# Decoder block on one core: the expert loop's gather in bf16 parts, norm weights behind it, residual in the last block

## The reference

```python
h = h + token_mixer(rmsnorm(h, norm_mix_w), ...)
xn = rmsnorm(h, norm_ffn_w)
logits = xn @ w_router + b_router
top_v, top_i = lax.top_k(logits, 4); gates = softmax(top_v)
# for each expert e, over the tokens routed to it:
hgu = x_e @ w_gate_up[e] + b_gate_up[e]          # 1024 -> 2048
act = min(g, 7) * sigmoid(1.702 * min(g, 7)) * (clip(u, -7, 7) + 1)
y_e = act @ w_down[e] + b_down[e]                # 1024 -> 1024
h = h + sum over experts of gate * y_e
out = rmsnorm(h, norm_final_w)[:, 16:]
```

## Time and profile before

| | |
|---|---|
| median of 3 executions | 1346.57 us |
| the profiled execution, its device time | 1345.64 us |
| its span, first to last instruction | 1343.9 us |
| TensorE matmul busy | 1329.1 us (99%) |
| VectorE busy | 567.4 us (42%) |
| ScalarE busy | 287.4 us (21%) |
| HBM read | 466.41 MB |
| granted TensorE clock, mean | 0.997 |

### The profile page before, as it was taken

How to read it: one execution, slowest core, us unless ns; L and a number is a source line. 1 busy time by engine, 2 the same in 40 slices (tenths; PEclk the granted TensorE clock), 3 DMA queues, 4 the chain that set the end, 5 groups by cost and what they waited for, 6 DMA issues and landing times.

```text
span 1343.9 us, 20286 instructions
## 1 busy us (share of the span) xinstructions
PE 1329.1 (99%) x8121; PEld 785.9 (58%) x8121; DVE 567.4 (42%) x1101; ACT 287.4 (21%) x500; POOL 14.3 (1%) x33
## 2 busy tenths in 40 slices
PE   8999999999999999999999999999999999999997
PEld 8999889899985444444444454444444444444442
DVE  5897899875645232232222232222232222232222
ACT  5443344443541011011011011011011011011011
POOL 1000000000000000000000000000000000000000
PEclk9999999999999999999999999999999999999999
DMA  9653353356678899999999999999999999999993
GB/s 326 223 165 121 129 180 126 126 189 192 219 302 334 378 418 432 431 433 432 430 433 432 430 433 434 429 432 434 429 433 433 430 432 433 430 432 425 428 428 150
DMA packets 77159, 467.91 MB, mean 348 GB/s; under 512 B 4295, under 2 KB 62199, under 8 KB 63335
## 3 DMA queue, kind: packets, MB, share of 16 engines
q1 hardware_dynamic: 76736, 467.32, 84.9%
q10 hardware_dynamic: 391, 0.16, 0.0%
HBM read 466.41 MB, written 1.05 MB: 348 GB/s over the span
## 4 chain that ended last, share of the span: by engine, by line
PE 97%; DVE 1%; ACT 1%; ACTq 0%; issue 0%; DVEq 0%
PE pb L754 33%; PE pb L781 17%; PE pb L719 9%; PE pb L529 6%; PE pb L531 6%; PE pb L530 6%; PE pb L804 5%; PE pb L690 2%; PE pb L773 2%; PE pb L796 1%; PE pb L761 1%; PE pb L771 1%; PE pb L494 1%; PE pb L614 1%; PE pb L616 1%; PE pb L615 1%
## 5 line engine op out<-in xcount | busy, mean ns | idle before, releaser
L1542 DVE TENSOR_SCALAR work<-pb 64x512 f32<-64x512 f32 x64 | 43.7, 683 | 480.7 <-PE pb L761 480.7
L754 PE MATMUL pb<-work,ubuf 128*64 128x512 f32 x992 | 218.1, 592 | 0.0
L529 PE MATMUL pb<-parts,whi 128*128 128x256 f32 (+1 forms) x640 | 185.3, 290 | 0.7 <-DVE parts L1137 0.7
L531 PE MATMUL pb<-parts,wlo 128*128 128x256 f32 (+1 forms) x640 | 182.5, 285 | 0.0
L530 PE MATMUL pb<-parts,whi 128*128 128x256 f32 (+1 forms) x640 | 182.3, 285 | 0.0
L754 PEld LDWEIGHTS pb<-work,ubuf 128*64 128x64 f32 x992 | 70.3, 137 | 132.9 <-issue 132.8
L1126 DVE TENSOR_TENSOR wlo<-work,whi 128x1024 fp32r<-128x1024 f32 x104 | 126.4, 1219 | 49.7 <-ACT whi L908 49.5
L908 ACT ACTIVATE whi<-work 128x1024 fp32r<-128x1024 f32 x104 | 109.4, 1057 | 135.6 <-PE pb L531 107.0
L781 PE MATMUL pb<-work,ubuf 128*64 128x512 f32 x576 | 130.6, 595 | 0.1
L754 PE MATMUL pb<-late_w,ubuf 128*64 128x512 f32 x576 | 126.7, 592 | 0.0
L719 PEld LDWEIGHTS pb<-onehot,hw 128*128 128x128 f32 x992 | 113.1, 192 | 19.4 <-issue 19.4
(11 more groups left out here) (235 smaller groups left out, 1324.2 us busy)
## 6 DMA issues: line engine op xcount, KB each, us to landing
work<-in_w_gate_up SPq DMA_DIRECT2D x28, 4096.0 KB, 21.6
split_w<-in_w_gate_up SPq DMA_DIRECT2D x15, 4096.0 KB, 21.1
late_w<-in_w_gate_up SPq DMA_DIRECT2D x14, 4096.0 KB, 21.1
work<-in_w_down SPq DMA_DIRECT2D x14, 4096.0 KB, 17.9
work<-in_w_in SPq DMA_DIRECT2D x40, 1024.0 KB, 5.2
late_w<-in_w_down SPq DMA_DIRECT2D x7, 4096.0 KB, 18.4
split_w<-in_w_down SPq DMA_DIRECT2D x7, 4096.0 KB, 18.7
late_w<-in_w_gate_up SPq DMA_DIRECT2D x8, 2048.0 KB, 17.7
```

The source lines that it names most:

```text
L529: pe.matmul(o, wh, xh, start=first, stop=False)
L531: ins = pe.matmul(o, wl, xh, start=False, stop=last)
L754: ins = pe.matmul(pb[u * SLOTS:(u + 1) * SLOTS, bank, :], xT[:, 2 * i + k, :], w[:, k, u * HID:(u + 1) * HID], start=(i == 0 and k == 0), ...
L1542: dve.tensor_scalar(hg, pb[0:SLOTS, 4 + s, :], LIMIT, None, ALU.min).then_inc(min_rdy, 1)
```

## The change

1. `hw` is kept as three bf16 parts whose sum is the float32 value: x3[0] = bf16(hw), x3[1] = bf16(hw - x3[0]), x3[2] = the rest. The loop's `gather` uses the three parts and a bf16 one-hot matrix: 6 matmuls into each of 8 column ranges in place of 2, all in bf16. The parts are made in the front by ScalarE (`first_part`, `second_part`) and VectorE (`rest_of`, `third_part`). `gather_first` stays in float32.
2. The norm's weights are no longer in `hw`. They are multiplied in behind the gather, in the copy from PSUM (`tokens`, now a multiply with `fnw`), and for block 0 by two more multiplies. The DMA that broadcasts these weights and VectorE's multiply with them (L1389) are gone.
3. `hidden(0)` of block 0 starts its first two chunks when the first half of `xT` is ready (`xh_rdy`).
4. The residual matmuls move from ahead of the loop to the last block, behind `down_bias`. The first scatter clears the banks instead.
5. The two matmuls that count tokens (L811, L812) move ahead of `gather_first(1)`, in the place of two of the matmuls that only keep TensorE busy.
6. The first four blocks are written out; TensorE's loop over known blocks has 6 rounds instead of 7.
7. The last `w_down` pair of 2 MB is two loads of 1 MB, each with its own semaphore.
8. The last scatter signals after each token tile, and ScalarE squares tile 0 as soon as that is there.

```diff
-            sp.dma_start(nwb[:, 0, :], a["norm_ffn_w"][0:1, :].to_broadcast([P, D])).then_inc(nwb_in, 16)
...
-            reload(rounds, 6, el, w_dn, 2)
+            sp.wait_ge(w_used, LOADS * rounds + (FIXED * LOADS - 2 * AHEAD + 6 + 2))
+            for i in range(2):
+                sp.dma_start(place_at(AHEAD + 6 + i), expert_src(el, w_dn, 0)[:, (2 + i) * 2 * D:(3 + i) * 2 * D]).then_inc(end_in[i], 16)
...
             def gather():
 
                 for k in range(KC):
-                    for t in range(TT):
-                        ins = pe.matmul(pb[:, 7, k * SLOTS:(k + 1) * SLOTS], hw[:, t, k * P:(k + 1) * P], onehot[:, t, :],
-                                        start=(t == 0), stop=(t == TT - 1))
+                    for n in range(3 * TT):
+                        ins = pe.matmul(pb[:, 7, k * SLOTS:(k + 1) * SLOTS], x3[:, n % 3, n // 3, k * P:(k + 1) * P],
+                                        onehot[:, n // 3, :], start=(n == 0), stop=(n == 3 * TT - 1))
                 ins.then_inc(gathered, 1)
...
+            def add_residual():
+                for t in range(TT):
+                    for c in range(2):
+                        pe.matmul(pb[:, 2 * t + c, :], ident[:, :], hx[:, t, c * 512:(c + 1) * 512],
+                                  start=False, stop=False, skip_group_check=True)
+
-            def scatter(stop):
+            def scatter(start=False, stop=False):
+
                 for t in range(TT):
                     for c in range(2):
                         rows = slice(c * SLOTS, (c + 1) * SLOTS)
                         ins = pe.matmul(pb[:, 2 * t + c, :], hotT[rows, t * P:(t + 1) * P], ysb[rows, :],
-                                        start=False, stop=stop, skip_group_check=True)
+                                        start=start, stop=stop, skip_group_check=True)
+                    if stop:
+                        ins.then_inc(acc_done, 1)
                 return ins
...
             pe.wait_ge(table_done, 4)
-            pe.wait_ge(h2_done, 4)
-            for t in range(TT):
-                for c in range(2):
-                    pe.matmul(pb[:, 2 * t + c, :], ident[:, :], hx[:, t, c * 512:(c + 1) * 512],
-                              start=True, stop=False, skip_group_check=True)
...
+            def first_part(t):
+                sc.wait_ge(xf_rdy, t + 1)
+                sc.activation(x3[:, 0, t, :], hw[:, t, :], ACT.Copy).then_inc(x3_rdy, 1)
+
+            def second_part(t, of):
+                sc.wait_ge(xr_rdy, 2 * t + 1)
+                sc.activation(x3[:, 1, t, :], of, ACT.Copy).then_inc(x3_rdy, 1)
...
+            def rest_of(t, to, parts):
+
+                dve.wait_ge(x3_rdy, parts)
+                dve.tensor_tensor(to, hw[:, t, :], x3[:, 0, t, :], ALU.subtract).then_inc(xr_rdy, 1)
+
+            def third_part(t, of, parts):
+                dve.wait_ge(x3_rdy, parts)
+                dve.wait_ge(xr_rdy, 2 * t + 1)
+                dve.tensor_tensor(x3[:, 2, t, :], of, x3[:, 1, t, :], ALU.subtract).then_inc(xr_rdy, 1)
...
             def tokens(n):
                 dve.wait_ge(gathered, n)
-                dve.tensor_copy(xT, pb[:, 7, :].rearrange("p (k n) -> p k n", n=SLOTS)).then_inc(xt_rdy, 1)
+                dve.tensor_tensor(xT, pb[:, 7, :].rearrange("p (k n) -> p k n", n=SLOTS), fnw(0, KC), ALU.mult).then_inc(xt_rdy, 1)
...
+            rest_of(1, hw[:, 1, :], 3)
             further_blocks()
+            third_part(1, hw[:, 1, :], 4)
```

More of the change, by code:

```diff
@@ L223, in build_block @@
         e_in = [sem(f"e_in{s}") for s in range(PLACES // 4)]
+        end_in = [sem(f"end_in{i}") for i in range(2)]
         l_in = [sem(f"l_in{s}") for s in range(LOADS // 2)]
@@ L710, in _ @@
             pe.matmul(pb[:, 1, 0:NE], before[:, :], mask[:, 1, :], start=False, stop=True).then_inc(rank_done, 1)
-            keep_busy(2, 2)
+            pe.matmul(pb[:, 0, NE:2 * NE], ones[:, :], mask[:, 0, :], start=True, stop=False, skip_group_check=True)
+            pe.matmul(pb[:, 0, NE:2 * NE], ones[:, :], mask[:, 1, :], start=False, stop=True,
+                      skip_group_check=True).then_inc(rank_done, 1)
             gather_first(1, 3, 0).then_inc(first_done, 1)
@@ L740, in first_unit, with hidden @@
                 return place_at(n)
-            def hidden(s, at, n0, sel, n=None, tokens=None):
+            def hidden(s, at, n0, sel, n=None, first=False):
                 bank = 4 + s
@@ L747, in hidden @@
                     pe.wait_ge(clip_rdy, n)
-                if tokens is not None:
-                    pe.wait_ge(xt_rdy, tokens)
                 for i in range(4):
+                    if first and i == 0:
+                        pe.wait_ge(xh_rdy, 1)
+                    if first and i == 2:
+                        pe.wait_ge(xt_rdy, 1)
                     w = at(n0 + i).rearrange("p (k n) -> p k n", k=2)
@@ L809, in _, with first_half @@
             pe.wait_ge(zeroed, 1)
-            pe.matmul(pb[:, 0, NE:2 * NE], ones[:, :], mask[:, 0, :], start=True, stop=False, skip_group_check=True)
-            pe.matmul(pb[:, 0, NE:2 * NE], ones[:, :], mask[:, 1, :], start=False, stop=True,
-                      skip_group_check=True).then_inc(rank_done, 1)
-            hidden(0, first_unit, 0, 1, tokens=1)
+            hidden(0, first_unit, 0, 1, first=True)
             pe.wait_ge(table_done, 4)
-            pe.wait_ge(h2_done, 4)
-            for t in range(TT):
-                for c in range(2):
-                    pe.matmul(pb[:, 2 * t + c, :], ident[:, :], hx[:, t, c * 512:(c + 1) * 512],
-                              start=True, stop=False, skip_group_check=True)
             rounds = pe.value_load(nblocks[0:1, 0:1], min_val=NE - 1 - FIXED, max_val=MAXB - 2 - FIXED)
             last = pe.value_load(nblocks[0:1, 1:2], min_val=NE - 1, max_val=MAXB - 2)
-            def first_half(b, at, more):
+            def first_half(b, at, more, first=False):
                 hidden(1, at, 0, b + 1, 2 * b + 1)
@@ L827, in first_half @@
                     pe.wait_ge(hot_rdy, 2 * b + 4)
+                    if first:
+                        pe.wait_ge(xr_rdy, 4)
                     gather()
@@ L830, in first_half @@
                 pe.wait_ge(y_rdy, b + 1)
-                scatter(False).then_inc(scat_done, 1)
+                scatter(start=first).then_inc(scat_done, 1)
                 pe.wait_ge(min_rdy, 2 * b + 2)
@@ L839, in first_half @@
                 down_bias()
+                if not more:
+                    add_residual()
             def second_half(b, at, n0):
@@ L848, in second_half, with whole @@
                 down(1, at, n0 + 2, 1)
-            def whole(b, at):
-                first_half(b, at, True)
+            def whole(b, at, first=False):
+                first_half(b, at, True, first)
                 pe.wait_ge(gslot_rdy, b + 1)
@@ L854, in whole @@
                 second_half(b, at, 8)
-            with pe.Fori(0, FIXED // 4) as g:
+            for j in range(4):
+                whole(j, fixed_unit(0, j), first=(j == 0))
+            with pe.Fori(0, FIXED // 4 - 1) as g:
                 for j in range(4):
-                    whole(4 * g + j, fixed_unit(g, j))
+                    whole(4 * g + (4 + j), fixed_unit(g, 4 + j))
             with pe.Fori(0, rounds) as i:
                 whole(i + FIXED, later_unit(i))
-            first_half(last, later_unit(rounds), False)
-            second_half(last, later_unit(rounds), 4)
+            first_half(last, last_unit(rounds), False)
+            second_half(last, last_unit(rounds), 4)
             pe.wait_ge(hotT_rdy, last + 2)
             pe.wait_ge(y_rdy, last + 2)
-            scatter(True).then_inc(acc_done, 1)
+            scatter(stop=True)
         @block.scalar
@@ L1049, in _ @@
             normalize(0)
+            first_part(0)
             evacuate(1, 0)
+            second_part(0, rest)
             square_half(1)
@@ L1439, in _ @@
             dve.tensor_scalar(stat[:, 14:15], stat[:, 2:3], 1.0 / D, EPS, ALU.mult, ALU.add).then_inc(half_done, 1)
+            rest_of(0, rest, 1)
             choose(0)
+            third_part(0, rest, 2)
             settle(0)
```

49 lines of the change are left out of this document (30 added, 19 removed).

## The result

The changed kernel takes 1338.93 us (median of 5 executions, 1337.53 to 1341.32) against 1346.36 us of the kernel before (median of 5, 1345.65 to 1346.72): a ratio of 0.9945 [0.9931, 0.9960], 0.55% faster. The profiled execution took 1337.71 us, its span 1335.8.

A forecast was written before the change was run, and what follows sets the result against it. The prediction took the DMA stream of weight loads, 29.18 us a block, as the bound once TensorE's reserve is used up. Terms -7.6 and -1.0 sum to -8.6, giving 1338.0 us, range 1334.8 to 1342.3.

The forecast's parts named there:

- Two clocks, the stream the slower: Loop: loads need 29.18 us a block, TensorE 28.84; TensorE's work counts only until its reserve is gone, then the stream's start.
- Gather 2.98 us: Loop's gather: 48 bf16 pairs at 62 ns take 2.98 us a block instead of 3.71, saving 0.73.
- weights cost nothing: Rival on the gather's bf16 pairs: stream starts up to 1.7 us earlier, total 1336.3 to 1336.9; chance 0.12.
- TensorE 28.1 a block, waits of about 1.1 from block 14: Loop: TensorE uses 1.07 us of reserve a block, then waits a little over 1 us at each hidden(1).
- Residual's removal 3.5: Start, block 0: residual's 3.63 us gone, 3.5 counted as saved, up to 1 less if register reads show.
- 0.37 earlier for hidden(0): Start, block 0: hidden(0) needs only the first half of xT, so begins at about 408.95 instead of 409.32.
- its result is needed only behind the scatter: Loop, tokens as a multiply from PSUM: costs about what the copy did, needed only behind scatter (1.99 us) and transposes.
- 4.6 earlier for the stream: Loop's start: load issued at 441.86 goes 0.37 + 3.5 + 0.73 = 4.6 us earlier, and all landings behind it.
- Residual at the end +3.43, less 0.43 and 0.25 for two waits that go: Last block: residual adds 3.43 us; waits ahead of first down chunk (0.43) and second turn_act (0.25) are saved.
- Tail 1.0: Kernel's end: last scatter releases tile 0 at its half, so ScalarE's squares start sooner, 1.0 us saved.
- a pair of 81 ns: Rival on the gather: it takes 3.89 us, 0.18 longer, 31 times, total 1350.1; chance 0.07.
- the late one-hot rows: Rival at the start: register reads exposed and one-hot rows or parts late, 1 to 3.5 us, 1339 to 1341.5; chance 0.09.

The follow-up runs named there:

- e11: Changed kernel with 128 instead of 64 moving columns in 42 of the gather's 48 matmuls, same instruction count: 1339.32 us.
- e4: Changed kernel with only 7/8 of each 4 MB load from the sixth on, the rest stale: 1276.73 us.
- e5: Changed kernel with VectorE copying the gathered tokens before the second activation instead of after it: 1339.31 us.
- e3: Changed kernel with every gather matmul done twice, the second time over the first: 1348.58 us.
- e2: Changed kernel with the residual's matmuls back ahead of the loop: 1337.86 us.
- e6: Changed kernel with the residual's matmuls in block 3 instead of the last block: 1338.34 us.
- e9: Changed kernel with one signal after the whole last scatter instead of one a token tile: 1340.26 us.
- e10: Changed kernel with two more passes of 48 bf16 pairs ahead of each gather, one with 16 moving, one with 64 stationary columns: 1419.84 us, one run.

## Why the prediction was right, step by step

The total came out as forecast: 1338.93 against 1338.0, inside the range, and 1337.71 against 1337.0 for the profiled execution. Its main reading held, some of its terms did not. The profiled execution is also closer than it has earned: its span is 8.1 us shorter, but 0.7 of that is a mixer that ended earlier. From h0 to the end the change gave 7.2, where the forecast's terms come to 8.2; most of the missing 1.0 is at the end, below.

- *Two clocks, the stream the slower.* Shown. 29.13 us a block; late `hidden(1)` start at their landings; 34 us more of work cost nothing (e11), an eighth less DMA gave 61 (e4). Landings come 9.71 us apart whether a load has been queued for 15 us or for 31.
- *Gather 2.98 us.* Wrong: 1.51. The step that failed is the column rate, "so bf16 saves 0.42 a column": I carried a rate from a 64-column load to a 128-column one, and the two do not lie on one rate (98 ns for 128 columns against 113 for 64 in one kernel). By the measured 98 the same working gives 116 - 94 = 22 ns, under the floor of 27. The rival "weights cost nothing" was the truth about the pair. I gave it 0.12 though its rule was at hand; a row at another width could not refute it.
- *Therefore TensorE 28.1 a block, waits of about 1.1 from block 14.* Wrong in size by the same step: 26.63, waits of about 2 us in rows and 2.5 by the time of a block, from block 7 (606.85) on. It cost nothing, as the forecast's own logic says that beyond the reserve nothing counts.
- *Residual's removal 3.5.* 3.76; the register reads are hidden under `hidden(0)`.
- *0.37 earlier for hidden(0).* About 0.15, counted from the first gather's records. The rest of the 0.86 between the two profiles is a mixer that ended earlier in that execution.
- *"its result is needed only behind the scatter", so `tokens` costs nothing.* Wrong for block 0: 1.27 us (e5 removes them). I checked when TensorE would need the result, and not what stands ahead of it on VectorE. The gather came 4.7 us earlier (422.77 for 427.42), while VectorE's one-hot rows, behind its added work in the front, came 2.0 later (420.20 for 418.23).
- *4.6 earlier for the stream.* From h0 on, the forecast has 3.5 + 0.73 = 4.23 of it, and the traces 4.65 (`w_down` landed 46.14 after h0 before, 449.95 - 408.46 = 41.49 now), made up of 3.76 for the residual and 2.2 for the gather less the wait of 1.27. At B 4.2 of them are left, as the changed kernel has more of the late landings named above (e3). Two errors cancelled, a gather that gave 1.5 more and a wait that took 1.3: the number was right to a part by luck.
- *Last pair at 1307.4, scatter at 1311.1, first down chunk at 1317.7.* 1306.94, 1310.76, 1317.78.
- *Residual at the end +3.43, less 0.43 and 0.25 for two waits that go.* The residual takes 3.63 (1314.15 to 1317.78), and from the first scatter to the last are 15.69 us against 12.26: 3.43 more, not 2.75; e2 and e6 give the same 3.4. The credit for the waits was the step that failed. Ahead of `down` 0.2 were saved and not 0.43. The 0.81 ahead of the second `turn_act` stands in the changed kernel as it did before:

```profile
1319.65 0.29 PEld L790 LDWEIGHTS pb<-ident,work 64*128 64x128 f32 x2 [0.81 <-issue]
```

  It is a pause of the weight loads alone, with matmuls running beside it. From the first `down` matmul to this `turn_act` are 1.87 us in both kernels, so it never lengthened the path.
- *Tail 1.0.* 0.83 from the two profiles, 0.9 to 1.07 by e9.

The other rivals are out: a pair of 81 ns is not seen, neither at the gather's 64 moving columns (31.5) nor at 128 (58, e11), and the late one-hot rows did not show (the gather ran with no wait at 422.77, the one-hot rows were ready at 420.62; 2.15 of cover).

Open ends. How the code loads slow the weight stream, and why by a step of 1.5 us at every eleventh load when a pass has twelve, no run here tells. Not tried by themselves are the start of `hidden(0)` at the first half of `xT`, the norm weights behind the gather, the first four blocks written out, and the last `w_down` pair in two loads; what is said of these rests on the traces of the two kernels alone.

## What to carry to other kernels

When an engine and the DMA stream are nearly level, read both per block and the reserve between them: once it is used up, an engine's saving is worth nothing, and only the stream's start and what stands behind its last landing count. Put work that must be done anywhere (here the residual) into the stretch with a reserve, not ahead of the stream's start nor behind its end (2.7 us here), and let early loads start in pieces. A pause of the weight loads is not a pause of the path: look whether the matmuls stop too. When work is moved earlier on one engine, check the other engine's list ahead of the result that it needs, not only the time at which it needs it.

## What the runs showed of the hardware

- A load of 128 bf16 columns lasts 98 ns and one of 64 lasts 113, and pairs with 64 moving columns follow at 31.5 and 34.2 ns (e10). With 128 stationary and 128 moving columns they follow at about 58 (e11): the moving side sets the pace.
- A loop body that outgrows TensorE's store of instructions (some 1,790 records a pass; 1,410 still fit) is loaded in each pass: stalls of 2 to 3 us (e3), up to 5.7 in the kernel with three passes of pairs (e10), and a slower weight stream.
- In one steady stream on one queue, 4 MB loads land 9.71 us apart (431 GB/s in the late window above), whether a load is queued for 15 us or for 31.
- A wait can cost more than itself, and give it back. Behind a wait of 2.89 us, the `hidden(1)` at 606.85 took 8.78 us instead of 7.04; the granted clock in it was 0.81, so that part of it ran at 1.2 GHz and not 2.4. The row of that window:

```profile
606.85:615.63 8.78, 8.78 (x34) 3.29 (x34) 0.00 (x0) 0.00 (x0) 0.00 (x0) 0.81 1.01 437
```

  The next wait was 0.62 instead of 1.9: a stream that is the bound hides the slow clock as well. Of the 26 waits at `hidden(1)` three were followed by such a row.
